# More landing places for loads, and another order of work at the phase ends of a two-block transformer kernel

## The reference, cut to what matters

```python
# block 1
h = rms_norm(x, g_mix_pre);  proj = h @ w_in          # attention, gated recurrence, two gates
merged = sigmoid(gate_a) * (y_attn @ w_attn_branch) + sigmoid(gate_b) * (y_hgrn @ w_hgrn_branch)
x = x + rms_norm(merged @ w_out, g_mix_post)
gate, up = split(rms_norm(x, g_ffn_pre) @ w_gate_up)
x = x + rms_norm((silu(gate) * up) @ w_down, g_ffn_post)
x = x + rms_norm((p @ w_ple_proj) * sigmoid(rms_norm(x, g_ple_pre) @ w_ple_gate), g_ple_post)
# block 2, for l in 0, 1
shift, scale, gate = split(silu(c) @ w_ada[l] + b_ada[l])
h = layernorm(x) * (1 + scale) + shift
u, z_f, cq, ckv, k_r, z_a = split(h @ w_in_2[l])      # Fourier mix of u, latent attention
y = concat(fourier(u, w_fmix[l]) * silu(z_f), attention * silu(z_a)) @ w_out_2[l]
x = layernorm(alpha * x + gate * y, ln_g[l], ln_b[l])
```

## Time and profile before

| | us |
|---|---|
| three runs | 2352.24, 2358.62, 2359.35 |
| median | 2358.62 |
| the profiled execution's own time | 2350.27 |
| its span | 2348.2 |
| TensorE busy | 2236.2 (95%) |
| VectorE busy | 1511.5 (64%) |
| ScalarE busy | 1107.2 (47%) |
| DMA, mean over the span | 213 GB/s |

### The profile page before, as it was taken

How to read it: one execution, slowest core, us unless ns; L and a number is a source line. 1 busy time by engine, 2 the same in 40 slices (tenths; PEclk the granted TensorE clock), 3 DMA queues, 4 the chain that set the end, 5 groups by cost and what they waited for, 6 DMA issues and landing times. The chain is left out here.

```text
span 2348.2 us, 27105 instructions
## 1 busy us (share of the span) xinstructions
PE 2236.2 (95%) x10514; PEld 1849.5 (79%) x10514; DVE 1511.5 (64%) x1883; ACT 1107.2 (47%) x1541; POOL 40.7 (2%) x66
## 2 busy tenths in 40 slices
PE   8999999999898999999999999997999997999997
PEld 6788888887676777777787777786888885788886
DVE  5665467757766777667777777765545556545556
ACT  5466455443334433444433334575545544545543
POOL 1000000000000000000000000000000000000000
PEclk9999999999999999999999999998999998999999
DMA  6543654368875888888888888773544474544463
GB/s 222 184 136 126 197 171 153 112 205 299 277 257 203 289 291 278 282 292 289 289 287 279 287 292 284 257 239 117 155 148 138 146 256 135 162 135 142 145 239 137
DMA packets 232768, 500.64 MB, mean 213 GB/s; under 512 B 15728, under 2 KB 24224, under 8 KB 231488
## 3 DMA queue, kind: packets, MB, share of 16 engines
q1 hardware_dynamic: 229168, 483.53, 62.8%
q0 software_dynamic: 3328, 14.88, 1.8%
q10 hardware_dynamic: 144, 0.51, 0.1%
HBM read 496.74 MB, written 2.12 MB: 212 GB/s over the span
## 5 line engine op out<-in xcount | busy, mean ns | idle before, releaser
L234 DVE TENSOR_TENSOR wl<-raw,wh 128x1024 fp32r<-128x1024 f32 (+2 forms) x696 | 835.8, 1208 | 583.7 <-ACT wh L230 578.0
L230 ACT ACTIVATE wh<-raw 128x1024 fp32r<-128x1024 f32 (+2 forms) x696 | 723.6, 1048 | 877.3 <-PE bank L213 297.7
L213 PE MATMUL bank<-wh,hh 128*128 128x512 f32 (+1 forms) x1616 | 642.9, 398 | 45.1 <-DVE wl L234 24.3
L213 PE MATMUL bank<-wh,hl 128*128 128x512 f32 (+1 forms) x1616 | 628.8, 389 | 0.0
L213 PE MATMUL bank<-wl,hh 128*128 128x512 f32 (+1 forms) x1616 | 628.6, 389 | 0.0
L213 PE MATMUL bank<-wh,ah 128*128 128x512 f32 (+1 forms) x1168 | 460.5, 394 | 18.5 <-DVE wl L234 15.6
L213 PE MATMUL bank<-wh,al 128*128 128x512 f32 (+1 forms) x1168 | 453.1, 388 | 0.0
L213 PE MATMUL bank<-wl,ah 128*128 128x512 f32 (+1 forms) x1168 | 453.1, 388 | 0.0
L213 PEld LDWEIGHTS bank<-wh,hh 128*128 128x128 f32 x1616 | 306.1, 189 | 118.6 <-DVE wl L234 37.1
L213 PEld LDWEIGHTS bank<-wh,hl 128*128 128x128 f32 x1616 | 305.9, 189 | 63.4
L213 PEld LDWEIGHTS bank<-wl,hh 128*128 128x128 f32 x1616 | 306.5, 190 | 58.1
(11 more groups left out here) (110 smaller groups left out, 976.7 us busy)
## 6 DMA issues: line engine op xcount, KB each, us to landing
raw<-in_w_in SPq DMA_DIRECT2D x264, 512.0 KB, 3.9
raw<-in_w_ada SPq DMA_DIRECT2D x192, 512.0 KB, 4.9
raw<-in_w_gate_up SPq DMA_DIRECT2D x176, 512.0 KB, 4.9
raw<-in_w_out SPq DMA_DIRECT2D x96, 512.0 KB, 4.8
raw<-in_w_down SPq DMA_DIRECT2D x88, 512.0 KB, 5.3
raw<-in_w_ple_gate SPq DMA_DIRECT2D x32, 512.0 KB, 4.5
raw<-in_w_attn_branch SPq DMA_DIRECT2D x16, 512.0 KB, 5.3
raw<-in_w_hgrn_branch SPq DMA_DIRECT2D x16, 512.0 KB, 5.6
```

The costliest lines, as they stand in the source:

```text
L213: return put("pe", lambda e: e.matmul(o, l, r, start=start, stop=stop_, skip_group_check=skip), w, sig, size(r) / 2400.0 * (4 if r.dtype = ...
L230: return e.activation(o, i, f, scale=scale, **k)
L234: return put(eng, lambda e: e.tensor_tensor(o, a, b, op), w, cost=vcost(eng, o))
```

## The change

1. **Landing places.** The fixed cycle of four becomes a list `raws` of free places, first in, first out, each with its semaphore key and what its next load must wait for. `lend_raw` appends 4 KB pieces of the arena that are idle in a stage; `end_raw` takes them back and returns what their new owner must wait for.

```diff
-            slot = i % NRAW
-            rel = raw_rel[i - NRAW] if i >= NRAW else None
+            buf_, key, rel = raws.popleft()
@@ gates, n == 2
                 g_rel[0] = now()
+                lend_raw((8, 12, 16, 20, 24, 28), g_rel[0])
@@ ev_post of "wo"
-            rel = now() if n == 0 else None
+            if n == 0:
+                y_rel.extend(end_raw((16, 20, 24, 28)))
+                y_rel.extend(now())
+                lend_raw((40, 44, 48, 52, 60), y_rel)
+            rel = y_rel
@@ before "gate"
-        g_free, u_free = [[], []], [[], []]
+        g_free, u_free = [[], []], [end_raw((8, 12)) for _ in range(2)]
@@ before "pproj"; ev_p waits for e_rel
+        e_rel = end_raw((40, 44, 48, 52, 60))
```

```diff
-    mixing = [n for n, b in enumerate(blocks) if b[0] in ("wa", "wh", "wo", "gate", "up", "down")]
+    gates = [n for n, b in enumerate(blocks) if b[0] == "gates"]
+    mixing = gates[6:] + [n for n, b in enumerate(blocks) if b[0] in ("wa", "wh", "wo", "gate", "up", "down")]
```

3. **Held subtractions.** In the second pass of a `split="last"` block, `take_item(hold=True)` issues load and rounding copy of the next block's first two units, and keeps the two `wl` subtractions back. `flush(1)` issues one and `flush()` the rest, inside the last evacuation:

```diff
@@ ev_pg_last
             done(t)
+            if m:
+                flush(1)
             t = tt(YR[:, m, cs], G[:, m, :], E_[:, m, cs], ALU.mult, t, e_tok[3], prel)
             t1 = sq_sum(G[:, m, :], YR[:, m, cs], SS[:, m, 3:4], t)
+            if m:
+                flush()
+                held_out[0] = True
             t = tt(YR[:, m, cs], YR[:, m, cs], GR[:, cs], ALU.mult, t1, t_row)
```

5. **Operand chunk ahead of splits.** `block(..., whole=True)` for the first "gate", "pgate" and "u" block of a phase:

```diff
+            if whole:
+                until(lambda: operand.tok[kts[0]] is not None)
```

More of the change, by code:

```diff
@@ L481, in program @@
         ptr = [0]
-        raw_rel = []
+        raws = deque((RAW[:, i, :], f"w{i}", None) for i in range(NRAW))
         split_tok = []
@@ L485, in program, with lend_raw, end_raw @@
         unit_slot = []
+        def lend_raw(places, rel):
+            for o in places:
+                raws.append((kb(o, 4), f"r{o}", list(rel)))
+        def end_raw(places):
+            toks, keep = [], [r for r in raws if r[1] not in [f"r{o}" for o in places]]
+            for r in raws:
+                if r[1] in [f"r{o}" for o in places]:
+                    toks += r[2]
+            raws.clear()
+            raws.extend(keep)
+            return toks
         def lend(op, end):
@@ L526, in ada_reduce, with flush, take_item @@
             mod_tok[l, c] = t
-        def take_item():
+        held = []
+        held_out = [False]
+        def flush(n=9):
+            while held and n:
+                held.pop(0)()
+                n -= 1
+        def take_item(hold=False):
             i = ptr[0]
@@ L538, in take_item @@
                 src = WORK[wn][row0 + k * P:row0 + (k + kk) * P, n0:n0 + nw].rearrange("(c p) n -> p c n", p=P)
-                raw = RAW[:, slot, 0:kk * nw]
-                t = dma("sp", raw.rearrange("p (c n) -> p c n", c=kk), src, f"w{slot}", [rel])
+                raw = buf_[:, 0:kk * nw]
+                t = dma("sp", raw.rearrange("p (c n) -> p c n", c=kk), src, key, [rel])
                 sl = slots.popleft()
@@ L543, in take_item, with low @@
                 th = act(wh, raw, ACTF.Copy, t, sl[2])
-                tl = tt(wl, raw, wh.bitcast(F32), ALU.subtract, th, sl[2])
                 unit_slot.append(sl)
-                raw_rel.append(tl)
-                split_tok.append(tl)
+                def low():
+                    tl = tt(wl, raw, wh.bitcast(F32), ALU.subtract, th, sl[2])
+                    raws.append((buf_, key, [tl]))
+                    split_tok.append(tl)
+                if hold:
+                    held.append(low)
+                else:
+                    assert not held
+                    low()
             else:
@@ L550, in take_item @@
                 src = WORK[f"w_ada_2@{l}"][k * P:(k + 1) * P, c * 1024:(c + 1) * 1024]
-                raw = RAW[:, slot, :]
-                t = dma("sp", raw, src, f"w{slot}", [rel])
+                raw = buf_
+                t = dma("sp", raw, src, key, [rel])
                 buf = (ada_n[0] // 16) % 2
@@ L569, in program, with block @@
         CCOL = COLS[:, 48:64]
-        def block(name, operand, kts, evac, *args, early=None, split=None, borrow=None):
+        def block(name, operand, kts, evac, *args, early=None, split=None, borrow=None, between=None, whole=False):
             nm, wn, row0, nk, n0, nw = blocks[bi[0]]
@@ L603, in block @@
                     n += stream[ptr[0]][0] == "g"
-                    take_item()
+                    take_item(hold=split == "last" and ms == (1,))
                 for q in range(kk):
@@ L632, in block @@
             if split:
-                at_once(evac(acc, t, done, 1, *args))
+                g = evac(acc, t, done, 1, *args)
+                if between is not None:
+                    while not held_out[0]:
+                        step(g)
+                        step_all()
+                    held_out[0] = False
+                    between()
+                at_once(g)
+                flush()
             elif evac is not None:
@@ L1376, in program @@
         y_tok = {}
+        y_rel = []
         def ev_post(acc, tok, done, n):
-            rel = now() if n == 0 else None
+            if n == 0:
[3 more added lines that the diff above has]
+            rel = y_rel
             t_row = hg_tok["row"]
@@ L1514, in program @@
             for c in range(p0, p1):
-                block("gate", Y, ALL, ev_gate, c)
+                block("gate", Y, ALL, ev_gate, c, whole=c == 0)
                 block("up", Y, list(range(16)), ev_up, c, 4 * (c - p0))
@@ L1533, in program @@
         e_tok = {}
+        e_rel = end_raw((40, 44, 48, 52, 60))
         def ev_p(acc, tok, done, n):
             for m in range(2):
-                t = cp(E_[:, m, n * 512:(n + 1) * 512], acc[m][:, :], tok, eng="act")
+                t = cp(E_[:, m, n * 512:(n + 1) * 512], acc[m][:, :], tok, e_rel, eng="act")
             e_tok[n] = t
@@ L1661, in program @@
         for n in range(3):
-            block("pgate", Y, ALL, ev_pg, n, borrow=last_of(H, 24) if n == 1 else None)
+            block("pgate", Y, ALL, ev_pg, n, whole=n == 0, borrow=last_of(H, 24) if n == 1 else None)
         until(lambda: (0, 5) in mod_tok)
         clear(H)
-        block("pgate", Y, ALL, ev_pg_last, split="last")
-        mix_now(0)
+        block("pgate", Y, ALL, ev_pg_last, split="last", between=lambda: mix_now(0))
         def layer(l, tk):
@@ L1924, in stat2 @@
                 return ST[:, 166 + o:166 + o + n]
-            block("u", H, ALL, ev_u, 0)
+            block("u", H, ALL, ev_u, 0, whole=True)
             block("u", H, ALL, ev_u, 1)
@@ L2057, in layer @@
             clear(H)
-            block("wo2", Y, ALL, ev_o_last, split="last")
-            if l == 0:
-                mix_now(1)
+            block("wo2", Y, ALL, ev_o_last, split="last", between=(lambda: mix_now(1)) if l == 0 else None)
         layer(0, mixd[0])
```

## The result

| | us |
|---|---|
| before, 4 runs beside it | median 2358.79 (2352.24 to 2359.35) |
| changed kernel, 4 runs | median 2277.28 (2275.59 to 2280.62) |
| ratio | 0.966, 95% interval 0.964 to 0.968 |
| profiled execution of the changed kernel, span | 2277.13, 2275.0 |

The account below looks back on a forecast made before the run. Took four landing places, not the DMA engines, to set the load rate (287 GB/s) that makes TensorE wait. 18 + 11 + 2 + 7.1 + 1.5 + 0.4 = 40 us off 2358.6 gave 2318 us, range 2307 to 2330.

Parts of the forecast that it names:

- the phase ends: Pauses around "gate", "pgate" and "wo2": operand chunk, held subtractions and mixes were to save 7.1, 1.5 and 0.4 us.
- part 5: Operand chunk scaled ahead of splits: 2.8 us saved before each layer's "u", 1.5 before "gate"; bounds together 0 and 8.
- the hold after "wo2": Holding subtractions lets the last evacuation after "wo2" start sooner, gain 1.9 us; with "pgate" +1.5, bounds -1 and 3.
- the mixes: At two ends, moving the mixes' copies readies the norm 0.2 us sooner each: 0.4 us, bounds 0 and 1.
- before "gate": Before the first "gate" matmul, the operand chunk could go ahead of two `wl` subtractions, saving 1.5 us.
- The new waits at the lending points: First loads into borrowed places wait for earlier work on SP's queue: 0, at worst 7.3 us each.
- no change of order can take back more than 112 us: Whole kernel: TensorE works 2236.2 of 2348.2 us, so reordering can regain at most 112 us.
- the term of 18 us: In 770 to 1521, more landing places make late loads vanish and take back 18 us; bounds 0 and 25.
- 11 + 2 us: In 550 to 728, 11 us of waits regained (bounds 0 and 15), plus 2 of lost clock (0 and 3).
- a fifth of the waits stays, since VectorE serves its queue in order: In 770 to 1521, a fifth of the 22.4 us of `wl` waits remains, with VectorE at 74% busy.
- the median is 8.4 us above this execution, so the forecast for the median is 2358.6 - 40: Whole kernel: the runs' median lies 8.4 us above the profiled execution, so 40 us saved gives a 2318 us median.
- nearly all idle time goes: Rival for the whole kernel: VectorE at 74% is no hindrance, gain 55 us, so 2303 us; chance 12%.

Follow-up runs that it names:

- experiment 1: Landing places alone added to the kernel before; items, held subtractions, mixes and operand chunk as before: 2285.83 us, ratio 0.971.
- experiment 3: The changed kernel with one borrowed landing place at a time (two in "wo") in place of five to seven: 2275.35 us, ratio 0.966.
- experiment 5: The kernel before with three landing places in place of four: 2629.81 us in two runs, ratio 1.118.
- experiment 10: The changed kernel with the splits of units 2 and 3 ahead of the operand's first chunk again: 2281.21 us, ratio 0.969.
- experiment 6: The changed kernel with every modulation item loaded a second time, unread, 192 more loads: 2330.47 us, ratio 0.991.
- experiment 7: The changed kernel with one more zero-adding VectorE sum after every second modulation item: 2275.42 us, ratio 0.967.
- experiment 2: Held subtractions, mixes and operand chunk added to the kernel before, without borrowed places and with items spread as before: 2346.38 us, ratio 0.996.
- experiment 4: The changed kernel without items moved into the gates blocks; the 192 modulation items start in "wa" as before: 2275.28 us, ratio 0.967.
- experiment 9: The changed kernel without the held subtractions: 2278.96 us, ratio 0.968.
- experiment 11: The changed kernel with the mixes issued after the row updates again: 2275.91 us, ratio 0.966.
- experiment 12: The changed kernel again, unaltered, on the same chip as the three runs before it: 2276.08 us, ratio 0.967.
- experiment 8: The changed kernel with one more zero-adding VectorE sum after every modulation item but each column's first: 2308.16 us, ratio 0.981.

## Why the prediction was wrong

**Right: what binds, and the phase ends.** Loads in four places set the rate at 285 GB/s; with more places TensorE's waits for `wl` vanish (experiments 1 and 3), with fewer they grow to 72 us (experiment 5). The phase ends came out as worked out: 2.8 us at each "u" for part 5 (2.8 and 2.8 in experiment 10), 1.9 against 1.7 for the hold after "wo2" and -0.4 against -0.2 to -0.3 after "pgate", 0.4 against 0.3 for the mixes, 1.5 before "gate" against 1.4 to 1.9. Sum 9.0 forecast, 8.6 to 9.1 found. The new waits at the lending points cost nothing, as said.

**Wrong, first step: "no change of order can take back more than 112 us", and every bound that came from idle time.** I took 26.7 us of idle TensorE in 770 to 1521, and 16.0 in 550 to 728, as all that late loads cost. The stage from "gate" to "pgate" shows what they did cost. Before, and after:

```profile
732.20:1532.90 800.70, 772.58 (x3437) 623.01 (x3437) 580.77 (x564) 333.06 (x380) 2.72 (x4) 1.00 0.84 280
```

```profile
709.50:1467.40 757.90, 756.42 (x3436) 628.06 (x3437) 572.68 (x558) 335.35 (x382) 2.73 (x4) 1.00 0.85 288
```

The same matmuls (3437 and 3436 records) take 42.8 us less, but the idle time falls only from 28.1 to 1.5, by 26.6. The other 16.2 us were in TensorE's busy time. How they come there is seen in one stall before:

```profile
1010.28 0.39 PE L213 MATMUL bank<-wh,hl 128*128 128x512 f32 x1
1011.94 0.50 PE L213 MATMUL bank<-wh,hh 128*128 128x512 f32 x1 [1.27 <-DVE wl L234]
1012.27 0.39 PE L213 MATMUL bank<-wl,hh 128*128 128x512 f32 x1
1012.50 0.40 PE L213 MATMUL bank<-wh,hl 128*128 128x512 f32 x1
```

In steady work a matmul starts every 0.227 us and is shown for 0.39, so each overlaps the next. (The profile records the start of a matmul and models its end.) Here 1.66 us pass from start to start where 0.227 were due, a loss of 1.43, and the idle time shown is 1.27. The matmul that ended the stall is shown for 0.50 and the next starts 0.33 after it, another 0.10. A stall shorter than 0.16 us is not shown at all.

Counted by starts over all of the stage: 3216 of its matmuls are 128x512 products with a weight. What their distances to the next start have above 0.227 us adds up to 47.4 us before and 6.0 after, a difference of 41.4 of the 42.8. Before, 144 distances are too long by over 0.05 us, 104 of them by less than 0.3; after, 39 are, 37 of them by less than 0.3. A rival would be that all matmuls run slower beside heavy loads or at a lower clock. The traces rule it out: the median distance is 0.227 us before, after and in experiment 6 at 375 GB/s, and the clock of the stage is 1.00 before and after. In experiment 5 the busy time of the same matmuls is 815 us, there in part at a lower clock. From "wa" to "gate" it is 189.3 us before and 181.0 after: 8.2 us more, some 3 of them at half clock.

So the step that failed is the price of late loads: the term of 18 us (bounds 0 and 25) for 770 to 1521 measured 42.8 over "gate" to "pgate", and 11 + 2 us (bounds 15 and 3) for the stretch before measured 23.7, without the pause before "gate".

**Wrong, second step: "a fifth of the waits stays, since VectorE serves its queue in order".** I left 8.7 us in 770 to 1521 and 5 in 550 to 728. Nothing stayed, and in experiment 7 nothing did at 86% or 93% either. `take_item` runs two to three units ahead, 5.5 us or more; that is enough for bursts of two 1.2 us instructions, and I had priced those as if it were not. (My "85% busy without TensorE's pauses" for 550 to 640 was also misread: 68.3 of 78.4 us are 87%. The changed kernel shows 82%.)

**Wrong, third step: "the median is 8.4 us above this execution, so the forecast for the median is 2358.6 - 40".** I carried the offset over. The changed kernel's profiled execution is 0.2 us from its median. Where the 8.4 us lay is not shown, as only two executions of that order of work have a trace; what they show points at the stage with late loads. It took 800.7 us in one and 808.8 in the other (experiment 2, whose order differs there only at the first "gate" block), but 757.2 to 758.4 in the changed kernel and in experiments 1, 3, 4, 7, 9, 10, 11 and 12. Part of the 8.4 is the scatter of the medians themselves: over all its runs here the kernel before lies between 2347.0 and 2362.1 us, the changed kernel between 2274.8 and 2280.8, and on the chip of experiment 12 the medians differ by 78.0 us in place of 81.5.

**The account.** Forecast for the stages with items: 18 + 11 + 2 = 31 us. Measured: 42.8 + 25.6 less the 1.9 of the pause before "gate", 66.5. Of the 35 missing, 14 are the waits that I left in place (8.7 + 5.0), and about 22 are stalls inside the busy time (16.2 + 8.2, less the 2 that I had for the clock). The offset of the median adds 8.4, and of the rest the start (+2.9) went the other way, within what that stretch does from run to run (518.6 to 526.8 in the runs with the change or a part of it). The rival nearest to the result was "nearly all idle time goes", with 55 us; it had the cause and the same wrong bound.

## What to carry to other kernels

Count what late data costs an engine from the starts of its instructions, or from the length of a stage against its instruction count at the steady pitch; idle time between pipelined instructions leaves out part of every stall and all short ones. A ring of landing places gives places x bytes / (landing + every step until release): if that product is the measured rate, one more place may be enough, and the rest of the memory can be kept. Where loads are on the path, expect a stage to scatter from one execution to the next (800.7 and 808.8 us here, against 757.2 to 758.4 in nine traces without).

## What the runs showed of the hardware

- The 16 DMA engines held 398 to 400 GB/s for loads of 512 KB with 4 KB per partition, at a busy share of 1.0 and a landing time of 9.6 us (experiment 6); at 300 GB/s the share was 0.89 and the landing time 5.2 us (the changed kernel), at 225 GB/s the landing time was 4.5 us (experiment 5).
- A matmul of 128x512 `fp32r` starts 0.227 us after the one before it at a clock of 1.00 and is shown for 0.39 us; of a stall the first 0.16 us, and the 0.10 us by which the next matmul was late after it, were shown as busy (kernel before, 1010 to 1013 us).
- Neither VectorE's nor ScalarE's instructions got slower at the higher rate: `wl` took 1224 ns before and 1224 ns after (the group with sources in the arena), `wh` 1061 and 1061, and in experiment 6 at 375 GB/s 1224 and 1061 again.
- VectorE at 93% busy over 90 us and at 86% over 660 did not hold up TensorE (experiment 7), with loads, copies and subtractions issued two to three units ahead; at 96 to 98% it did (experiment 8).
